# Feed-forward gate and up units as seven block products in place of eight, and hidden parts of 6, 6, 6 and 4

## The reference

```
def swiglu(x, w_gate, w_up, w_down):
    return (silu(x @ w_gate) * (x @ w_up)) @ w_down      # w_gate, w_up: 1024 x 2816, w_down: 2816 x 1024

h = h + 0.5 * swiglu(rmsnorm(h, ffn1_norm), ffn1_w_gate, ffn1_w_up, ffn1_w_down)
...  # latent attention and gated delta net, merged
h = h + 0.5 * swiglu(rmsnorm(h, ffn2_norm), ffn2_w_gate, ffn2_w_up, ffn2_w_down)
return rmsnorm(h, final_norm)[:, 16:]
```

## Time and profile before

| | us |
|---|---|
| median of 3 runs | 2114.69 |
| lowest, highest | 2111.71, 2115.12 |
| span of the profiled execution | 2111.5 |
| PE, PEld busy | 2059.4, 1769.5 |
| DVE, ACT, POOL busy | 817.3, 736.1, 761.0 |

### The profile page before, as it was taken

How to read it: one execution, slowest core, us unless ns; L and a number is a source line. 1 busy time by engine, 2 the same in 40 slices (tenths; PEclk the granted TensorE clock), 3 DMA queues, 4 the chain that set the end, 5 groups by cost and what they waited for, 6 DMA issues and landing times.

```text
span 2111.5 us, 32172 instructions
## 1 busy us (share of the span) xinstructions
PE 2059.4 (98%) x13992; PEld 1769.5 (84%) x13992; DVE 817.3 (39%) x1300; ACT 736.1 (35%) x1140; POOL 761.0 (36%) x243
## 2 busy tenths in 40 slices
PE   8999999999999999999999999999999999999998
PEld 6899888878977789999999878798777788888886
DVE  4400675145357655220222242266566644211222
ACT  5332222336556544221222344342312323222222
POOL 4433232545310054334333431045243235434432
PEclk9999999999999999999999999999999999999999
DMA  5323122222310122223323431222013223223322
GB/s 173 100 87 109 52 74 80 80 90 81 100 61 21 41 80 81 81 75 106 100 66 94 103 100 31 60 68 81 22 62 111 81 82 98 90 83 107 100 68 72
DMA packets 170052, 171.52 MB, mean 81 GB/s; under 512 B 16940, under 2 KB 160680, under 8 KB 169912
## 3 DMA queue, kind: packets, MB, share of 16 engines
q1 hardware_dynamic: 168508, 167.25, 25.1%
q10 hardware_dynamic: 1404, 2.23, 0.3%
HBM read 163.17 MB, written 6.29 MB: 80 GB/s over the span
## 4 chain that ended last, share of the span: by engine, by line
PE 89%; DVE 4%; issue 3%; ACT 2%; POOL 1%; DMA 1%; ACTq 0%; SPq 0%; DVEq 0%; POOLq 0%
PE ps L2101 87%; PE ps L2103 2%; DMA x_rows<-in_x 0%; ACT diag L927 0%; DVE gdn_x L1966 0%; DVE gdn_inv_t L1949 0%; POOL w_lo L758 0%; POOL stat L775 0%; ACT u_hi L953 0%; DMA ret_decay<-c_decay 0%; ACT w_hi L899 0%; ACT residual L952 0%; DVE gdn_inv_t L1945 0%; DVE tmp L1414 0%; DVE sg L1609 0%
## 5 line engine op out<-in xcount | busy, mean ns | idle before, releaser
L758 POOL TENSOR_TENSOR w_lo<-w_raw,w_hi 128x2048 fp32r<-128x2048 f32 (+3 forms) x153 | 654.8, 4282 | 901.7 <-ACT w_hi L899 896.2
L2101 PE MATMUL ps<-u_hi,w_hi 128*128 128x512 f32 (+1 forms) x1904 | 584.4, 347 | 9.8 <-DVE sg L1609 2.6
L2101 PE MATMUL ps<-u_hi,w_lo 128*128 128x512 f32 (+1 forms) x1904 | 578.6, 344 | 0.0
L2101 PE MATMUL ps<-u_lo,w_hi 128*128 128x512 f32 (+1 forms) x1904 | 569.5, 344 | 1.0 <-DVE u_lo L1402 0.8
L2101 PEld LDWEIGHTS ps<-u_hi,w_hi 128*128 128x128 f32 x1904 | 328.6, 189 | 53.0 <-issue 5.5
L2101 PEld LDWEIGHTS ps<-u_lo,w_hi 128*128 128x128 f32 x1904 | 326.6, 189 | 43.7 <-DVE u_lo L1402 5.5
L2101 PEld LDWEIGHTS ps<-u_hi,w_lo 128*128 128x128 f32 x1904 | 328.1, 189 | 40.0 <-issue 0.5
L899 ACT ACTIVATE w_hi<-w_raw 128x2048 fp32r<-128x2048 f32 (+3 forms) x157 | 279.0, 1779 | 175.0 <-PE ps L2101 168.9
L2101 PE MATMUL ps<-hidden_hi,w_hi 128*128 128x264 f32 (+1 forms) x528 | 141.1, 321 | 0.0
L2101 PE MATMUL ps<-hidden_lo,w_hi 128*128 128x264 f32 (+1 forms) x528 | 141.0, 322 | 0.0
L2101 PE MATMUL ps<-hidden_hi,w_lo 128*128 128x264 f32 (+1 forms) x528 | 140.8, 321 | 0.0
(11 more groups left out here) (379 smaller groups left out, 2959.8 us busy)
## 6 DMA issues: line engine op xcount, KB each, us to landing
w_raw<-in_w_in_a SPq DMA_DIRECT2D x22, 1024.0 KB, 5.3
w_raw<-in_ffn_w_gate SPq DMA_DIRECT2D x22, 1024.0 KB, 5.4
w_raw<-in_ffn_w_up SPq DMA_DIRECT2D x22, 1024.0 KB, 5.4
w_raw<-in_w_in SPq DMA_DIRECT2D x17, 1024.0 KB, 5.2
w_raw<-in_ffn_w_down SPq DMA_DIRECT2D x16, 768.0 KB, 4.2
w_raw<-in_ffn_w_down SPq DMA_DIRECT2D x16, 640.0 KB, 3.9
w_raw<-in_w_out_a SPq DMA_DIRECT2D x8, 1024.0 KB, 5.0
w_raw<-in_w_kv SPq DMA_DIRECT2D x8, 1024.0 KB, 5.4
```

The source lines that it names most:

```text
L758: pool.tensor_tensor(WL[:, u % RAWS, part], RAW[:, u % RAWS, part], WH[:, u % SPLITS, part].bitcast(F32), ALU.subtract).then_inc(lo_done, 1)
L2101: return nc.tensor.matmul(o, a, b, start=start, stop=stop, **kw)
```

## The change

Take a unit's weight as four blocks B11, B12 (k-tiles 0 to 3; first and second 128 columns), B21, B22 (k-tiles 4 to 7), and the input as four blocks A (first or second half of the tokens, k-tiles 0 to 3 or 4 to 7). The four output blocks need eight block products. The change forms them from seven (p1 to p7), each 4 k-tiles x 3 matmuls over half the tokens, 84 matmuls in place of 96 of half the tokens (48 of all in ffn2). For that:

- per unit, DVE makes four sums of weight blocks (`w_sums`: three into TF, one in place in RAW), ScalarE and GpSimd split three of them beside the unit (`seven_hi`, `lo`);
- per feed-forward, DVE makes four sums of input blocks (`mix_sums`, 16 instructions), which are split too (SH, SL, and one in place of the second half's first tiles in UH, UL);
- ScalarE copies p1 out of PSUM (FIRSTP), and DVE joins the products (`seven_out`).

The first two units of each feed-forward stay as they were, 20 take the new way. The hidden parts are 6, 6, 6 and 4 tiles, each with 4 down units over all its tiles. Semaphores of several loads are merged to make room. At the core of the diff:

```diff
-FFN_PARTS = (12, 10)
+FFN_PARTS = (6, 6, 6, 4)
+ORDER = ("p1", "p5", "p6", "p7", "p2", "p4", "p3")
+FIRST_ORDER = ("p1", "p6", "p7", "p5", "p2", "p4", "p3")
...
-            ffns[name] = [(job(part, spread_after=3 if name == "ffn1" and part == FFN_PARTS[0] else None),
-                           job(8, fold=2, kc=part // 2)) for part in FFN_PARTS]
+            ffns[name] = [(job(part, spread_after=3 if name == "ffn1" and n == 0 else None), job(4, kc=part))
+                          for n, part in enumerate(FFN_PARTS)]
...
+                if u in seven_no:                                        # GpSimd, lo(u)
...
+                    pool.wait_ge(sum_hi, 2 * v + 1)
+                    pool.wait_ge(w_summed, 4 * v + 3)
+                    pool.tensor_tensor(WL[:, a, 0:half], RAW[:, a, 0:half], WH[:, b, 0:half].bitcast(F32),
+                                       ALU.subtract).then_inc(sum_lo, 1)
+                    pool.wait_ge(sum_hi, 2 * v + 2)
+                    pool.tensor_tensor(TL[:, e, :], TF[:, e, :], TH[:, e, :].bitcast(F32),
+                                       ALU.subtract).then_inc(sum_lo, 1)
+                    lo_part(u, slice(half, UNIT), u + 2)
...
+            def seven_hi(u):                                             # ScalarE, in the body of unit u - 1
...
+                act.wait_ge(w_summed, 4 * v + 2)
+                nc.scalar.activation(WH[:, b, 0:half], RAW[:, a, 0:half], ACT.Copy).then_inc(sum_hi, 1)
...
+                act.wait_ge(w_summed, 4 * v + 4)
+                nc.scalar.activation(TH[:, e, :], TF[:, e, :], ACT.Copy).then_inc(sum_hi, 1)
+                nc.scalar.activation(WH[:, b, half:UNIT], RAW[:, a, half:UNIT], ACT.Copy).then_inc(hi_done, 1)
...
+            def w_sums(u):                                               # DVE
...
+                nc.vector.tensor_tensor(t3, b12, b22, ALU.subtract).then_inc(w_summed, 1)
+                dve.wait_ge(w_summed, 4 * v + 1)
+                nc.vector.tensor_tensor(b12, b12, b11, ALU.subtract).then_inc(w_summed, 1)
+                dve.wait_ge(w_summed, 4 * v + 2)
+                nc.vector.tensor_tensor(t2, b12, b22, ALU.subtract).then_inc(w_summed, 1)
+                dve.wait_ge(w_summed, 4 * v + 3)
+                nc.vector.tensor_tensor(t4, b21, t2, ALU.add).then_inc(w_summed, 1)
...
+                    def seven_out(i, j):                                 # DVE; x, y, z, w: PSUM banks
...
+                        dve.wait_ge(prod, product_tick(u, "p6"))
+                        nc.vector.tensor_tensor(U2[:, low], FIRSTP[:, low], y, ALU.add).then_inc(joined_done, 1)
...
+                        nc.vector.tensor_tensor(U3[:, low], U2[:, low], w, ALU.add).then_inc(joined_done, 1)
...
+                        nc.vector.tensor_tensor(dst[:, 1, high], U3[:, low], z, ALU.add).then_inc(joined_done, 1)
...
+                        dve.wait_ge(prod, product_tick(u, "p2"))
+                        nc.vector.tensor_tensor(dst[:, 0, low], factor(0, low), x, ALU.mult).then_inc(ps_free[s0], 1)
+                        dve.wait_ge(prod, product_tick(u, "p4"))
+                        nc.vector.tensor_tensor(dst[:, 0, high], U2[:, low], w, ALU.add).then_inc(joined_done, 1)
...
+                        nc.vector.tensor_tensor(dst[:, 0, high], dst[:, 0, high], factor(0, high),
+                                                ALU.mult).then_inc(chunk_ready, 1)
+                        dve.wait_ge(done, unit_ticks[u])
...
+                        nc.vector.tensor_tensor(dst[:, 1, low], U2[:, low], z, ALU.add).then_inc(ps_free[s1], 1)
...
+                        nc.vector.tensor_tensor(dst[:, 1, 0:width], dst[:, 1, 0:width], factor(1, slice(0, width)),
+                                                ALU.mult).then_inc(chunk_ready, 1)
...
                         for m in range(2):                               # after the outputs: scale, or hidden_lo
...
+                            if m == 0:
+                                w_sums(u + 2)
...
+                    if name == "p2":                                     # TensorE, seven()
+                        pe.wait_ge(lo_done, u + 2)
+                        pe.wait_ge(first_kept, v + 1)
+                    if name == "p4":
+                        pe.wait_ge(joined_done, 4 * v + 2)
+                    if name == "p3":
+                        pe.wait_ge(joined_done, 4 * v + 3)
+                    weights, moving, bank, first = made[name]
+                    for k in range(k4):
...
+                        mm(o, wh, xh, start=first and k == 0, stop=False, skip_group_check=not first)
+                        mm(o, wh, xl, start=False, stop=False, skip_group_check=not first)
+                        last = mm(o, wl, xh, start=False, stop=k == k4 - 1, skip_group_check=not first)
```

More of the change, by code:

```diff
@@ L321, in build, with order_of, product_tick, tiles_before @@
         n_units = at[0]
+        seven_units = [jg.unit0 + n for name in ("ffn1", "ffn2") for part, (jg, _) in enumerate(ffns[name])
+                       for n in range(jg.units) if part or n >= 2]
+        seven_no = {u: v for v, u in enumerate(seven_units)}
+        first_sevens = [ffns[name][0][0].unit0 + 2 for name in ("ffn1", "ffn2")]
+        def order_of(u):
+            return FIRST_ORDER if u in first_sevens else ORDER
+        def product_tick(u, name):
+            return 6 * seven_no[u] + order_of(u).index(name) + 1
+        def tiles_before(number, part):
+            return 22 * number + sum(FFN_PARTS[:part])
         row_slots = sorted((s % SLOTS for s in range(at_rows[1], at_rows[1] + NT)), key=lambda s: s == 0)
@@ L1140, in body @@
                                 nc.scalar.activation(HH[:, 4 * i + 2 * (j // 2) + m, 0:width], TMP[:, m, 0:width], ACT.Copy).then_inc(hh_done, 1)
+                        if part == 0 and (i, j) == (0, 0):
+                            for t in range(3):
+                                act.wait_ge(mixed, 8 * number + t + 2)
+                                nc.scalar.activation(SH[:, t, :, 0:half], SF[:, t, :, 0:half], ACT.Copy).then_inc(mix_hi, 1)
+                        if part == 0 and (i, j) == (0, 1):
+                            act.wait_ge(done, unit_ticks[u])
+                            nc.scalar.activation(UH[:, 0:k4, second_half], XS1[:, :, 0:half], ACT.Copy).then_inc(mix_hi, 1)
                     each(jg, body)
@@ L1680, in ffn_dve @@
+                        if part == 0 and (i, j) == (0, 1):
+                            c = slice(cols.start + half, cols.stop)
+                            dve.wait_ge(mix_hi, 5 * number + 5)
+                            nc.vector.tensor_tensor(UL[:, 0:k4, c], XS1[:, :, 0:half], UH[:, 0:k4, c].bitcast(F32),
+                                                    ALU.subtract).then_inc(mixed, 1)
                     each(jg, body)
                     def body(i, j):
[L1683 to L1696 removed]
@@ new lines, in body @@
+                        for m in range(2):
+                            k = 2 * j + m
+                            slot, uses = chunk_of(jd, i, j, m)
+                            dve.wait_ge(done, tick_of(jd, i, j, m))
+                            nc.vector.scalar_tensor_tensor(out=halves(RES[:, k, cols]), in0=acc(slot, width), scalar=0.5,
+                                                           in1=halves(RES[:, k, cols]), op0=ALU.mult,
+                                                           op1=ALU.add).then_inc(ps_free[slot], 1)
@@ L2424, in ffn_pe @@
                 for part, (jg, jd) in enumerate(ffns[name]):
-                    project(jg, UH, UL, cols, k_ready=(ul_done, applied[name]), after=None if part else name)
-                    project(jd, HH, HL, hcols, kc=FFN_PARTS[part] // 2,
-                            k_ready=(hl_done, 22 * number + (FFN_PARTS[0] if part else 0)))
+                    if part == 0:
+                        project(jg, UH, UL, cols, k_ready=(ul_done, applied[name]), after=name, units=range(2))
+                    for n in range(jg.units):
+                        if jg.unit0 + n in seven_no:
+                            seven(name, number, jg, n, cols)
+                    project(jd, HH, HL, hcols, kc=FFN_PARTS[part], k_ready=(hl_done, tiles_before(number, part)))
             ffn_pe("ffn1", 0)
```

244 lines of the change are left out of this document (197 added, 47 removed).

## The result

The changed kernel takes 2217.7 us (median of 4 runs, 2217.0 to 2222.4) where the kernel before takes 2114.8 (2111.7 to 2115.1): ratio 1.0496, interval 1.0481 to 1.0511. The forecast was 2219 and slower.

The account below looks back on a forecast made before the run. TensorE bounds the kernel before; after, GpSimd and two-SBUF-input DVE instructions excluding each other would. ffn1 +45.4 and ffn2 +58.9 give +104 on 2111.5, 2216; with 3.2 from span to median, 2219 us, range 2155 to 2250.

Parts of the forecast that it names:

- TensorE's saving turns into waits: Both feed-forwards: the 52.6 us of TensorE time saved by fewer matmuls would become waits, with TensorE busy in 90% of the span.
- The collision: Gate/up units: two-SBUF-input DVE instructions wait out GpSimd's splits, ending 0.55 us after them; a pair costs 4.61 + 0.41 us.
- A unit of 12.9 us: Steady seven-product unit: 12.9 us against 11.745 (ffn1) and 11.12 (ffn2), bounds 12.0 and 13.7.
- A part: Part of six units: 10.3 + 14.5 + 3 x 12.9 + 14.25 = 77.75 us, +7.3 in ffn1, +10.7 in ffn2.
- The first part: Start of each feed-forward, with input sums: by the part's end +25.8 us in ffn1, +30.3 in ffn2; bounds per start +9, +35.
- The four parts cost nothing: Down projections: four parts in place of two add 32 DVE adds of 0.7 us, hidden under 8.8 us units.
- The sum: Whole kernel: ffn1 +45.4 and ffn2 +58.9, together +104 us on the span of 2111.5.
- A: Rival: the port doesn't bind, TensorE bounds units at 10.27 and 9.96 us; 2086 us in all, chance 9%.
- B: Rival: the port binds less, 12.0 us a unit and half the start costs; 2160 to 2190 us, chance 17%.
- D: Rival: waits cancel the gain, units 12.9 us only where DVE is late, 11 elsewhere; 2110 to 2160 us, chance 5%.
- The signs: Trace signs expected, among them p1 starts 12.9 us apart inside parts, GpSimd near 65%, gaps over 20 us at the starts.
- two signs of being wrong: Wrong if weight sums beside a running w_lo last 0.7 us, or if units come under 11 us.

## Why the prediction was right

- **TensorE's saving turns into waits.** Right: with TensorE's 12 matmuls a unit put back, the time is the same. TensorE is busy in 93% of the span (90% expected), GpSimd in 57% and 56% of the feed-forward stretches (65% expected).
- **The collision, and DVE's waits to GpSimd's end.** Right, and with it the choice of 0.55 us after the end: 0.57 and 0.56 in the cycle shown. By the Trainium skill (SBUF — State Buffer, Who interferes with whom) a VectorE instruction with two SBUF inputs contends with a GpSimd instruction that reads SBUF, and not with one that only writes it. The trace agrees with both halves: 2.92 us beside GpSimd's subtraction, 0.70 with zeros written in its place.
- **A unit of 12.9 us.** 12.7 (ffn1) and 12.6 (ffn2) for a unit in the full cycle. The schedule by positions held. What failed is the reason put behind it, "GpSimd or a two-input DVE instruction runs all the time": it is true of the row, but no cause. Taking DVE's sums off the port gave 14 us of 103. The unit is as long as a loop in program order, in which two of DVE's two-input instructions are blocked; the second block, that of the last multiply, closes it.
- **A part.** The sum came out better than its terms. First unit 11.5 for 10.3, second about 15 for 14.5, third 11.4 to 11.6 in six parts for 12.9, and the last pair at 14.4 + 10.1 or 12.7 + 16.7 for 12.9 + 14.25. Parts of six took 75.6 and 80.0 us in ffn1 (77.75 predicted), the part of four 50.4 (52.0). The lower clock is in the 15.4 of a second unit (0.78) and in the 16.7 (0.80), and I had expected it in the starts alone. With the extra matmuls, at clock 1.00, the same first three units take 11.7, 13.1 and 12.7 us.
- **The first part.** ffn1: first seven-product unit at 845.5, 849.8 predicted; +23.8 at the part's end for +25.8. Two steps went otherwise. TensorE began p1 at 831.3 and not at 821.85, after a wait of 15.5 us: one of the unit's PSUM slots was still held by the second plain unit, whose output (L1836) stands behind the three low parts in DVE's order. That did not decide, since p5 had to wait for the last low part until 839.4 anyway. That low part ended 4.5 us before its 843.8, as it was held behind the first of the fourth unit's splits alone. In ffn2 the first one ends at 1836.3, 42.2 us after DVE's first output of the plain units, where the same step takes 38.1 in ffn1: a window from 1812.3 to 1843.0 has TensorE busy in 20.0 of 30.7 us and the clock at 0.68. That is most of what ffn2 costs over the prediction (+63.2 for +58.9); ffn1, up to DVE's first output in ffn2, is +45.9 for +45.4.
- **The four parts cost nothing.** Right, 1.0006.
- **The sum.** +109.1 between the two profiled spans, +103.0 between the medians, +104 predicted. The two differ by 6.1, of which 4.7 is that the profiled execution of after was the slowest of its four. The terms missed by 2 to 4 us each, in both directions, and largely cancelled. So the closeness of 2219 to 2217.7 is partly luck.
- **Rivals.** A needed a GpSimd that doesn't read. B's 12.0 us did not appear as the period of a steady unit. Units near D's 11 did: the third of six parts, at 11.4 to 11.6, but each behind one of about 15.
- **The signs.** p1's starts were not evenly 12.9 apart. Of the two signs of being wrong, weight sums beside a running w_lo lasted 2.74 us, not 0.7. But units under 11 us came twice, 10.1 at a part's end (997.2 and 2099.3 us), each behind one of 14.4: by its letter that sign was met, and it was put too narrowly, for the pair takes 24.5.

## What to carry to other kernels

Before moving work to idle engines, write one cycle of all engines in program order, with every two-SBUF-input DVE instruction held behind every long GpSimd subtraction; the busy shares (55% and 42% here) say nothing of it. Write the first and last units of a part too: most of what the experiments' forecasts missed lay there. Where DVE and GpSimd are both asked for elementwise work in one short cycle, count whether DVE alone can do it: here it is twice as fast for the same columns. Count its work in a window of one unit, without the neighbours' slack. Saved matmuls paid here only where the other engines had slack to prepare them: in every second unit, prepared beside work that is bound by TensorE.

## What the hardware showed that I had not expected

- GpSimd's subtractions hold a two-input DVE instruction to their end, but a GpSimd memset of 1024 or 1536 columns (0.955 and 1.39 us) holds nobody up.
- Not every GpSimd instruction on SBUF holds DVE. In the kernel before, the one of 5.42 us on 32 columns let three two-input DVE instructions through at 0.77 us each (1422.13). Beside a w_lo three of the same took 6.67 us (at 1414.19). Why was not tested:

```profile
1421.02 5.42 POOL L834 TENSOR_TENSOR gdn_small<-gdn_small,minus_half 128x32 f32<-128x32 f32 x1 [1.52 <-DVE gdn_small L1827]
```

- A two-input DVE instruction can slip in cheaply between two GpSimd instructions, as the schedule of the prediction had it: L1815, issued at 1069.08, took 0.49 us, and the GpSimd one recorded from 1069.24 took 2.59 in place of 2.40.
- TensorE's granted clock falls in single stretches: 0.80 over the last unit of ffn1's first part, 1.00 with the 12 matmuls more in it. In ffn1's parts of the changed kernel all five waits of 3.8 to 4.0 us come with a stretch at the lower of the two levels (1.2 and 2.4 GHz); of the five of 2.2 us, one does.
